# A hybrid decoder layer on one core: the next turn's q, k and v become the filling of an attention turn, and the first pair of the wide stage is computed plainly

## What is computed

```python
h = rms_norm(x, g_pre_mix)
cb, cc, ch, q, k, v, ga, gb = split(h @ w_in)      # 3 x 512, 3 x 512, 2 x 1024 columns
conv_u = causal_dwconv(cc * ch, conv_prev, w_conv_a)
y_a = (cb * conv_u) @ w_a
o = stick_breaking(q, k_all, v_all, sb_bias)       # 8 heads of 64; past keys and values in pages
merged = sigmoid(ga) * y_a + sigmoid(gb) * (o @ w_b)
x = x + rms_norm(merged @ w_o)
...                                                # a ConvFFN and a per-layer input embedding
```

## Time and profile before

| | |
|---|---|
| three runs | 1719.48, 1721.18, 1724.46 us; median 1721.18 |
| the profiled execution's own time | 1719.32 us |
| its span | 1717.6 us |
| mean granted TensorE clock | 0.993 |
| busy: PE, DVE, ACT, POOL | 97%, 69%, 48%, 21% of the span |
| opening; wide stage | 0 to 44 us; to 211 us |
| turns (slots) | q, k, v and slots, 114.5 us each, from 211 to 676 us |

### The profile page before, as it was taken

The page is one execution under the profiler, slowest core; times in us unless marked ns, Lnnn a source line. Parts: engine busy times, 40 slices in busy tenths (PEclk is TensorE's granted clock), DMA queues, the critical chain, the costliest instruction groups (busy, mean ns, idle before and its releaser), DMA issues.

```text
span 1717.6 us, 25950 instructions
## 1 busy us (share of the span) xinstructions
PE 1657.8 (97%) x8709; PEld 1416.9 (82%) x8709; DVE 1184.6 (69%) x1678; ACT 832.3 (48%) x1433; POOL 360.6 (21%) x291
## 2 busy tenths in 40 slices
PE   9699988999989989999999999999999999999998
PEld 8588887787887977998878888888888888888886
DVE  7965525537447257655878888888888798777566
ACT  7322235546456366214554444444444544465665
POOL 1144300000000000000116666666666100000100
PEclk9899999999999999999999999999999999999999
DMA  5112253131131221435222222222221863244333
GB/s 167 45 56 76 84 155 95 34 107 58 51 113 36 80 80 69 141 131 185 99 87 78 77 77 77 77 77 77 77 77 40 277 237 116 82 147 168 120 130 117
DMA packets 178314, 174.98 MB, mean 102 GB/s; under 512 B 17423, under 2 KB 144235, under 8 KB 178220
## 3 DMA queue, kind: packets, MB, share of 16 engines
q1 hardware_dynamic: 167274, 168.87, 30.3%
q10 hardware_dynamic: 10946, 4.91, 1.0%
HBM read 131.89 MB, written 41.84 MB: 101 GB/s over the span
## 4 chain that ended last, share of the span: by engine, by line
PE 61%; DVE 2%; issue 0%; ACT 0%; DMA 0%; POOL 0%; SPq 0%; DVEq 0%; POOLq 0%; ACTq 0%
PE pair L3595 10%; PE pair L3655 8%; PE pair L3656 8%; PE pair L3657 8%; PE pair L3793 4%; PE pair L3795 4%; PE pair L3794 4%; PE pair L3664 2%; PE pair L3116 2%; PE pair L3093 2%; PE pair L3091 2%; PE pair L3092 2%; PE pair L3603 1%; DVE left L2511 1%; PE pair L3779 1%; PE pair L3778 1%
## 5 line engine op out<-in xcount | busy, mean ns | idle before, releaser
L3164 PE MATMUL pair<-xh,wh 128*128 128x384 f32 (+1 forms) x600 | 209.0, 348 | 4.8 <-DVE qs L2451 4.5
L3166 PE MATMUL pair<-xh,wl 128*128 128x384 f32 (+1 forms) x600 | 197.3, 329 | 0.0
L3165 PE MATMUL pair<-xl,wh 128*128 128x384 f32 (+1 forms) x600 | 197.0, 328 | 0.0
L1195 POOL TENSOR_TENSOR hn<-hn 128x512 f32<-128x512 f32 x4 | 5.2, 1288 | 654.8 <-DVE hn L2645 654.8
L3164 PEld LDWEIGHTS pair<-xh,wh 128*128 128x128 f32 x600 | 114.2, 190 | 9.2 <-DVE qs L2451 4.8
L3793 PE MATMUL pair<-woph,foph 128*128 128x512 f32 x308 | 120.4, 391 | 0.0
L3795 PE MATMUL pair<-woph,fopl 128*128 128x512 f32 x308 | 119.9, 389 | 0.0
L3794 PE MATMUL pair<-wopl,foph 128*128 128x512 f32 x308 | 119.9, 389 | 0.0
L3165 PEld LDWEIGHTS pair<-xl,wh 128*128 128x128 f32 x600 | 114.3, 191 | 0.0
L3166 PEld LDWEIGHTS pair<-xh,wl 128*128 128x128 f32 x600 | 113.7, 189 | 0.0
L2195 DVE TENSOR_TENSOR wl<-raw,wh 128x1024 fp32r<-128x1024 f32 x33 | 40.4, 1224 | 70.9 <-ACT wh L1349 70.7
(11 more groups left out here) (529 smaller groups left out, 4847.8 us busy)
## 6 DMA issues: line engine op xcount, KB each, us to landing
rawp<-in_w_up SPq DMA_DIRECT2D x88, 256.0 KB, 3.8
wd<-in_w_down SPq DMA_DIRECT2D x55, 256.0 KB, 3.0
raw<-in_w_in SPq DMA_DIRECT2D x52, 256.0 KB, 3.4
f_spill<-cv SPq DMA_DIRECT2D x22, 552.0 KB, 2.8
f<-f_spill SPq DMA_DIRECT2D x44, 256.0 KB, 5.6
gat<-gate_spill SPq DMA_DIRECT2D x16, 544.0 KB, 4.4
x_spill<-x SPq DMA_DIRECT2D x16, 512.0 KB, 3.2
wraw<-in_w_in SPq DMA_DIRECT2D x28, 256.0 KB, 3.9
```

The source lines that it names most:

```text
L3164: t_.matmul(b, h, xhi, start=(k == 0), stop=False, skip_group_check=True)
L3165: t_.matmul(b, h, xlo, start=False, stop=False, skip_group_check=True)
L3166: ins = t_.matmul(b, l, xhi, start=False, stop=(k == KD - 1), skip_group_check=True)
```

## The change

It does four things.

1. **Pair 0 of the wide stage is plain** (`wide_plain`): four products of 8 steps (a and b for the first tile's two halves of the columns, S for the sample rows, c and d for the second tile's), 96 matmuls of 512 columns in place of 84. Its weight sums and the adding of its parts on DVE are gone. The sums of the input are still made, for pair 1, in the order shown; pair 1's weight sums (POOL) no longer wait for pair 0's.
2. **q, k and v of the next turn are filling.** Only turn 0 has them ahead of its slots (`first_turn`). Turns 0 to 2 have the jobs q, k, v of the next head pair and two gates, 120 steps over the 28 slots; turn 3 has six gates, 144 steps. `qs`, `ks2`, `kl` and `vn` have two sets. The next turn's `pk` is transposed at the end of slots 18, 20, 25 and 26, on another bank than before; its page scores come in slots 25 and 27.
3. **Results wait in DRAM.** The new buffers lie where `cout` and `oT` were. Three turns' results go through a small tile `ot` to `o_spill` (three ACT DMAs a turn), and `cout` and `oT` are loaded when the last turn's first gate is due.
4. **Ahead of turn 0**, ACT and DVE read q's first unit before they split the next job's weights, and SP loads those weights when two of the last wide pair's six gate DMAs have landed, not all.

```diff
+TURN_GATES = (2, 2, 2, 6)
+def jobs_of(c):
+    first = WIDE_GATES + sum(TURN_GATES[:c])
+    return ([(kind, c + 1) for kind in "qkv"] if c + 1 < NC4 else []) + [("g", first + i) for i in range(TURN_GATES[c])]
...
+PAST_AT = {18: 0, 20: 1, 25: 2, 26: 3}
...
-    return "1S267543" if n == 0 else "162S7543"
+    return "162S7543" if n else "abScd"
...
         @block.sync
-                    hold(d_wl, W_LOW["h1" if n else "c", n])
+                    hold(d_wl, W_LOW["h1", n])
                     wide_load(n + 1)
...
+                    if n == NW - 1:
+                        hold(wg_out, 96 * len(GATE_PAIRS) - 64)
+                        load(in_job(3))
...
+            for c in range(NC4):
+                gates = 0
+                for j in range(TURN_JOB[c], TURN_JOB[c + 1]):
+                    kind, m = JOBS[j]
+                    if j + 3 < IN_JOBS + 2:
+                        load(in_job(j + 3) if j + 3 < IN_JOBS else ab_job(j + 3 - IN_JOBS))
+                    if kind == "q":
+                        hold(p_past, 4 * m)
+                        keys(m, 0)
+                        keys(m, 1)
+                    if kind == "g" and gates == 0 and c + 1 < NC4:
+                        hold(p_x, 4 * (c + 1))
+                        for q in range(4):
+                            values(c + 1, q)
+                    if kind == "g" and gates == TURN_GATES[c] - 1 and c + 1 < NC4:
+                        hold(p_past, 4 * (c + 1) + 1)
+                        keys(c + 1, 2)
+                        hold(p_past, 4 * (c + 1) + 2)
+                        keys(c + 1, 3)
...
+                    if kind == "g":
+                        gate_out(m)
+                        gates += 1
...
         @block.scalar
+            def first_turn():
+                q_high(0, 2, 0)
+                act.wait_ge(wg_out, 96 * len(GATE_PAIRS))
                 whi()
+                for gr in range(1, NG):
+                    q_high(0, 2, gr)
...
+            def out_in(c, i):
+                half = STEPS[VALUES[i][0]][0]
+                if c + 1 < NC4:
+                    act.wait_ge(o_out, 48 * c + (32 if half else 0))
+                    dst = ot[:, 0:CW]
...
+                    if n and rows_after(c, n - 1):
+                        natural(c + 1, *rows_after(c, n - 1))
+                    if n and ended_in(c, n - 1)[1:] == ("k", NG - 1):
+                        k_twice(c + 1)
+                    if not last and n - 1 in PAST_AT:
+                        past_in(c + 1, PAST_AT[n - 1])
...
+                        if kind == "q":
+                            q_high(c + 1, j, gr)
+                        elif kind == "k":
+                            k_high(c + 1, j, gr)
+                        elif kind == "v":
+                            v_copy(j, gr)
+                        else:
+                            gate(j, gr)
...
         @block.vector
-            block_sums()
             wide_h(0, 0)
             wide_h(0, 1)
...
+            for t in kl:
+                for h in range(2):
+                    v.memset(f(t[h])[other(h), :], 0.0)
...
+                    if gr == 0:
                         wlo()
+                    if kind == "q":
+                        q_low(c + 1, TURN_JOB[c] + unit_ // NG, gr)
+                    if kind == "k":
+                        k_low(c + 1, TURN_JOB[c] + unit_ // NG, gr)
...
         @block.tensor
+            def past(c, q):
+                pe.wait_ge(pk_in[q % 2], pkn[q % 2].step(64))
+                pe.wait_ge(a_past, 4 * c + q)
+                pe.wait_ge(a_x, c + 1)
...
+                    if rows_after(c, n):
+                        new_rows(c + 1, *rows_after(c, n))
+                    if c + 1 < NC4:
+                        if n == 25:
+                            pages(c + 1, 0)
+                        if n in PAST_AT:
+                            past(c + 1, PAST_AT[n])
+                        if n == SLOTS - 1:
+                            pages(c + 1, 1)
+                            new_keys(c + 1)
```

More of the change, by code:

```diff
@@ L1525, in wide_sc, with plain @@
                 copied(s_.activation(wsb[:, :, :], wide_s_bank.rearrange("p (h n) -> p h n", h=2), ACT.Copy))
+            def plain(what):
+                i = "abcd".index(what)
+                act.wait_ge(p_wq, wide_done(0, what))
+                copied(s_.activation(wide0[i // 2][:, HALF * (i % 2):HALF * (i % 2) + HALF], plain_bank[what], ACT.Sigmoid))
             for n in range(NW):
@@ new lines, in v_copy, with gate, k_twice @@
+            def v_copy(j, gr):
+                s_.activation(part(vT[:, :], gr), unit_in(j, gr), ACT.Copy).then_inc(a_kv, 1)
+            def gate(j, gr):
+                b = unit_in(j, gr)
+                act.wait_ge(stg_out[gr], stn[gr].at())
+                s_.activation(stg[gr][:, 0:GROUPS[gr][1]], b, ACT.Sigmoid).then_inc(a_gt, 1)
+                stn[gr].step(16)
+            def k_twice(c):
+                act.wait_ge(a_qk, 1 + 2 * NG * (c + 1))
+                for h in range(2):
+                    s_.activation(ks2[c % 2][h][other(h), 0:SEQ], f(ks2[c % 2][h])[own(h), 0:SEQ], ACT.Copy)
@@ new lines, in sample_in @@
+            def sample_in(c):
+                act.wait_ge(p_xt, xn_.step())
+                src = xb_[:, 0:P].rearrange("p (b h q) -> p b h q", b=NB, h=2)
+                dst = ot[:, CW:CW + NS] if c + 1 < NC4 else oT[:, c, SEQ:TOK]
+                for h in range(2):
+                    rows = slice(64 * h, 64 * h + 64)
+                    ins = s_.activation(dst[rows, :].rearrange("p (b q) -> p b q", q=NT), src[rows, :, h, :], ACT.Copy)
+                ins.then_inc(a_x, 1)
+                if c + 1 < NC4:
+                    act.wait_ge(a_x, xn_.at(1))
+                    act.dma_start(o_spill[c:c + 1, :, SEQ:TOK].rearrange("o p t -> p (o t)"), dst).then_inc(o_out, 16)
@@ L1642, in pair, with slots @@
+            def slots(c, last):
                 for n in range(SLOTS):
+                    unit_, kind, gr = ended_in(c, n)
                     if n < NSTEP:
@@ L2483, in pair, with first_turn, slots @@
                     v.memset(k[:, 4 * P:4 * P + 1], 1.0)
+            def first_turn():
+                q_low(0, 2, 0)
+                wlo()
+                for gr in range(1, NG):
+                    q_low(0, 2, gr)
                 wlo()
                 for gr in range(NG):
-                    q_low(gr)
+                    k_low(0, 3, gr)
                 wlo()
-                for gr in range(NG):
-                    k_low(gr)
-                wlo()
-                qbn.step(2)
+            def slots(c, last):
+                biases(c)
                 for n in range(SLOTS):
```

699 lines of the change are left out of this document (354 added, 345 removed).

## The result

The changed kernel takes **1707.97 us** (median of 4 runs, 1706.90 to 1709.27) against 1720.62 us for the kernel before on the same chip: a ratio of 0.9924, 95% interval 0.9910 to 0.9939, some 13 us less. 1709.9 was forecast, in a range of 1688 to 1722. The profiled execution has a span of 1705.4 us, 12.2 less than before.

A forecast was written before the change was run, and what follows sets the result against it. TensorE, busy 1657.8 of 1717.6 us, bounds the kernel, with waits in opening, first turn and slots. Terms -2 - 7.4 - 6.0 - 18.4 + 10.5 + 12 = -11.3 gave 1709.9 us against the median of 1721.18; range 1688 to 1722.

The forecast's parts named there:

- opening: Wide stage's start: with pair 0 plain, pair 1 starts in effect at 80.9 instead of 82.36; -2 us, bounds -5 and +3.
- first turn: Ahead of turn 0: TensorE's 4.48 us wait at 219.9 and the half clock after it go; -7.4 us.
- last turn: Last turn's slots: six filling jobs remove nearly all of 6.6 us of waits, 0.6 left; -6.0 us.
- turns 0 to 2, idle removed: The three other turns: five filling jobs remove 6.6 us of waits each, less 1.4 for v rows; -18.4 us.
- (a): Slots: q and k units pass through ACT and DVE ahead of scan and product; 3.5 us a turn, +10.5.
- (b): Turn boundaries: TensorE waits 3 and 1 us for pk, issued behind a load awaiting DVE's low part; +12 us.
- turn 0's late load: Turn 0: job 6's load leaves behind values' 16 DMAs; the forecast had no term for it, 0.
- after the stage: From the first matmul with `ch` on, behind the turns; the forecast had no term for it, 0.
- Rival 2: Turn boundaries: longer page waits plus half clock, 9.9 us each, make the kernel slower, 1727.6 us; chance 0.1.
- Rival 1: Turns: the new waits are small, (a) 1 us a turn and (b) 0, giving 1690 us; chance 0.28.
- Rival 3: Turns: nothing gained, detour and page wait cost 6 us each a turn, giving 1723 us; chance 0.12.
- The turn's period: Sign in the profile: the forecast is wrong if a turn's period stays at 114.5 us or falls under 108.

The follow-up runs named there:

- e6: The kernel before with only the plain first pair and its order of sums and low parts: 1719.62 us, ratio 0.9985.
- e8: The kernel before with the first turn's order and cout's four transfers moved behind the turn's last load: 1715.11 us, ratio 0.9961.
- e5: The kernel after with gates dealt 3, 3, 3, 3 in place of 2, 2, 2, 6: 1715.88 us, ratio 0.9967 to the kernel before.
- e7: e3 with DVE taking q's and k's low parts one slot later, behind scan and product: 1678.27 us, ratio 0.9748 to the kernel before.
- e3: The kernel after with both page fetches earlier and job 6 loaded ahead of turn 0's values: 1690.76 us, ratio 0.9817 to the kernel before.
- e1: The kernel after with both page fetches, values and the last eight of pk, issued earlier: 1692.78 us, ratio 0.9827 to the kernel before.
- e9: The kernel before with only cout's four transfers moved behind the turn's last load: 1718.43 us, ratio 0.9985.
- e11: The kernel after with only pk's last eight DMAs issued earlier, behind values: 1714.35 us, ratio 0.9960 to the kernel before.
- e4: The kernel before with only the first turn's order (q's first unit ahead of the next weights, loaded earlier): 1722.93 us, ratio 1.0011.
- e10: The kernel after with only values' 16 DMAs issued earlier: 1709.34 us, ratio 0.9931 to the kernel before.
- e2: The kernel after with job 6's load ahead of values' 16 DMAs of turn 0: 1706.96 us, ratio 0.9906 to the kernel before.

## Why the prediction was right, and where its terms were not

The total was right within 2 us; its terms were less so, and that is in part luck. By the measured column the gains were 11 us larger than forecast and the costs 10 us larger, and the two cancelled.

| term | forecast | measured | by |
|---|---|---|---|
| opening | -2 | -2.1 (-0.3 to -4.6); -2.9 in the trace | e6 |
| first turn | -7.4 | -6.7; -5.7 in both traces, from q's first matmul to the scores of new keys (43.7 to 38.0) | e8 |
| last turn | -6.0 | -9.6 | windows; e5 |
| turns 0 to 2, idle removed | -18.4 | about -24, by difference | stage; e7's turns |
| (a) units' detour | +10.5 | +11.8 | e7 on e3 |
| (b) page wait | +12 | +15.9 | e1 |
| turn 0's late load | 0 | +3.2 | e3 on e1 |
| after the stage | 0 | -1.1 | trace |

The term by difference is what is left of the stage: -8.2 + 5.7 + 9.6 - 11.8 - 15.9 - 3.2 = -23.8. No run shows it by itself. The turns of e7, in which both costs are reordered away, agree with it: from one turn's scores of new keys to the next's they take 100.1, 94.3 and 94.3 us against 114.2, 114.5 and 114.0. Less one job each (11.8), and with 5.5 back in turn 0 for v's rows of two head pairs, they are 7.7, 8.4 and 7.9 us shorter, 24.0 in all. Of the 1.1 us after the stage, 0.8 is a wait for `adl` (DVE) at 900.80 that the kernel after doesn't have; e9 has 0.93 there and e11 0.73, so I don't put it down to the change.

**Opening.** Right: pair 1 starts at 78.81, where 78.7 was forecast, and of the half clock 3.4 us lie behind that start (80.4 to 83.8, granted clock 0.53), which cost 1.7 for the 2.2 that I took. TensorE's two waits came to 7.8 us for my 10, in part because the products between them ran at half clock (0.52 from 66.7 to 73.6). The forecast had DVE slowed by 1.4 us beside POOL. In the trace POOL's four subtractions lie at 45.6 to 55.6, and the DVE operations beside them took 2.92, 3.26 and 2.58 us where 2.28 is their time alone, 1.9 us in sum:

```profile
46.95 2.92 DVE L2448 TENSOR_TENSOR wsr<-wsr,xh 128x2048 f32<-128x2048 f32 x1
49.90 3.26 DVE L2449 TENSOR_TENSOR wsr<-wsr,xl 128x2048 f32<-128x2048 f32 x1
...
55.15 2.58 DVE L2433 TENSOR_TENSOR ws1l<-wsr,ws1h 128x2048 fp32r<-128x2048 f32 x1 [1.52 <-ACT ws1h L1505]
...
45.63 2.09 POOL L1244 TENSOR_TENSOR wtc<-wraw 128x512 f32<-128x512 f32 x1 [34.33 <-DMA wraw<-in_w_in]
47.79 3.22 POOL L1244 TENSOR_TENSOR wtb<-wraw,wtc 128x512 f32<-128x512 f32 x1
50.97 3.35 POOL L1244 TENSOR_TENSOR wtb<-wraw 128x512 f32<-128x512 f32 x1
54.28 1.31 POOL L1244 TENSOR_TENSOR wtc<-wraw,wtb 128x512 f32<-128x512 f32 x1
```

The 5.2 us that I had worked out from the Trainium skill's rule (SBUF - State Buffer, "Who interferes with whom") did not come. The rule says that whichever of the two issues first has the shared ports for its whole instruction and the other is blocked meanwhile, and the trace agrees with that. Each of the three DVE operations began while a subtraction ran, with 0.77, 1.11 and 0.44 us of it left, and took 0.64, 0.98 and 0.30 longer than alone. The middle two subtractions began with 2.08 and 2.19 us of a DVE operation left, and took 1.9 and 2.0 longer than the last, which began alone and took 1.3. What was wrong was my use of the rule: I let DVE lose four whole subtractions, and it lost only what was left of three, while POOL did most of the waiting.

**First turn.** The wait and its half clock went. Two waits of 0.96 (`pk`) and 1.06 us (`kl`) are left, for one of 0.32 before, which is the difference between 7.4 and 5.7 us; the forecast had `pk` land 0.7 us before it was wanted. The step that failed is a term left out: the forecast doesn't mention the `cout` transfers, and without their move the edit that I priced at -7.4 gives +2 (e4).

**Turns, what goes.** The mechanism was right and the size too small, since I took the idle time shown for the waiting. With three jobs the last turn's slots waited 7.2 us where 4.75 are shown (e5), and 9.6 in the kernel before, where I had 6.6.

**(a).** Right in kind and nearly in size: 3.5 a turn forecast, 3.4 measured in turns 1 and 2, 4.8 in turn 0. Of the single waits (0.6, 0.4, 1.1, 0.7, 0.7) the trace has 0.70, 0.42 and 0.67, and, ahead of the values, 1.54, which I had not listed.

**(b).** The chain is the one described: e10 shows that moving values alone changes nothing, and e11 that values are the next limit, 1.7 us behind. The first of the two waits measured 3.64, 3.54 and 3.19 for the forecast's 3; the second is under 0.3 for 1. What failed is that no half clock was counted: behind each wait it stood for 3.4 to 6.8 us. 15.9 / 3 = 5.3 a boundary instead of 4.

**Rival 2** named that half clock, and this part of it came true. Its waits, as long as the 4.48 us at 219.9 and longer, did not: they are 3.2 to 3.6 us, and 5.3 a boundary is under the 7.8 from which it would have decided. The Trainium skill (TensorE: Matmul & The Clock Gate, "HAM oscillation") warns that a wait for data between groups of matmuls can put the clock back each time. The kernel after agrees: with a wait of over 3 us at each boundary the clock fell at each, and with these waits gone (e1) it stayed up there. e2 and e10 each have a boundary where it didn't fall (see the last section). **Rival 1** (new waits small) was wrong of the change as made, but e7's 1678 shows the place it pointed to: with (a), (b) and the late load taken away by reorderings the kernel is faster than the 1690 it gave. **Rival 3** had the right shape, two costs against two gains, with both costs too high. The turn's period came out at 103 us, where I had written 107, and that I would be wrong under 108. By that sign the forecast is wrong; but neither number follows from my own sum. With a job less (11.8), 114.5 - 6.6 + 3.5 + 4 - 11.8 is 103.6, and that is what was measured.

## What to carry to other kernels

A list of DMAs on one queue is a schedule: price each edit by what leaves ahead of what, since a large transfer moved elsewhere can be worth more than the edit one meant to make (e4, e8), and half of a reordering can be worth nothing or less (e10, e11). Work that fills an engine's holes should stand behind, not ahead of, the operations that this engine owes to the critical loop (e7: 12 us for a few lines). Idle time in short stops understates what removing them gives, here by 1.5 times (7.2 for 4.75 us, e5).

## What was not expected of the hardware

Where the clock falls. Waits of 3.64, 3.54, 3.48 and 3.19 us in after were followed by half clock (for 6.8, 3.4, 3.4 and 3.4 us). In e10 a wait of 3.16 us, with another of 1.47 behind it, was not, while one of 3.50 in the same run was. Windows of e10 around the two (the clock is the third number from the end):

```profile
346.00:357.00 11.00, 6.38 (x44) 4.02 (x45) 0.00 (x0) 2.07 (x4) 0.00 (x0) 1.00 0.27 84
450.00:461.00 11.00, 8.08 (x40) 5.41 (x40) 0.00 (x0) 2.17 (x4) 0.00 (x0) 0.84 0.23 75
```

The wait of 2.06 us that e3 has at 263.6 left the clock up, too:

```profile
262.00:272.00 10.00, 7.96 (x51) 7.60 (x52) 5.94 (x14) 5.79 (x18) 0.00 (x0) 1.00 0.34 101
```

Shorter waits than these did bring it down, as in e5 (2.75 us) and e10 (2.98 us, with 0.6 behind it):

```profile
355.00:366.00 11.00, 8.25 (x47) 6.41 (x47) 0.00 (x0) 2.28 (x4) 0.00 (x0) 0.84 0.27 84
550.00:561.00 11.00, 7.39 (x44) 6.09 (x45) 0.79 (x8) 1.83 (x5) 0.00 (x0) 0.84 0.40 125
```

One of 2.92 in e5 did, too, while those of 2.57 and 2.61 in e5 and one of 3.04 in e2 did not. So between 2.6 and 3.2 us the length of a wait doesn't tell whether the clock falls. Where it falls, it costs 1.7 or 3.4 us beside the wait, which can be a part of the spread between executions of one kernel; no run shows that part by itself.

A job's weights (two DMAs of 256 KB) needed 3.9 us from issue to their reader behind `pk` alone (e8) and 9.2 us behind 2.1 MB of other transfers: the bytes ahead in the queue counted (e8 against e4), though their issues themselves took only 1.9 us.
